# Linear attention groups of a two-block network: one update product for both directions, scores between the updates, outputs beside the scans

## The chip, the cores and the metric

The kernel runs on one core of one Trainium2 chip. Its time is that of the whole program in device microseconds, the median of repeated runs. It is one long program: two layers of a first block (attention and a mixture of experts), then two layers of a second block. The change lies in the second block only.

## The reference, cut to what matters

Each layer of the second block has a mixer. One part of it is gated linear attention over 512 image tokens and 256 context tokens, 6 heads, keys of 32 and values of 64, computed forward and backward in time and added. Tokens are cut into chunks of 16. Decays `b` are running sums inside a chunk:

```python
q_dec = q * jnp.exp(b)
k_inv = k * jnp.exp(-b)
k_end = k * jnp.exp(b_last - b)
a = jnp.where(causal, jnp.einsum('bnihk,bnjhk->bnhij', q_dec, k_inv), 0.0)
o_intra = jnp.einsum('bnhij,bnjhv->bnihv', a, v)
def step(s, xs):
    qd, ke, vv, dec = xs
    o = jnp.einsum('bihk,bhkv->bihv', qd, s)
    s = s * dec[..., None] + jnp.einsum('bjhk,bjhv->bhkv', ke, vv)
    return s, o
```

So each chunk has an update of a 32x64 state per head, a scan runs over the 48 chunks, and a token's output is a part from its own chunk (scores times values) and a part from the state before the chunk. The second layer gives outputs for the 512 image tokens only, the first for all 768. Everything of this part is float32.

## The kernel before, in words

`gated_linear` (L2476) first computes the decayed tensors (`decays`, L2507), and then calls `gla_group` (L2593) twice, once for each three heads. With two layers there are four such groups. A group is a chain of blocks of instructions, and all engines meet at a barrier after each block (`end`, L137), so a group shares no time with what is before or behind it. SyncE issues nothing in a group.

A group of the kernel before has three blocks:

1. `transpose` (L170): `q_dec` and `k_inv` are turned by TensorE into `q_decT` and `k_invT`, tokens along the free axis.
2. The main block (L2641). TensorE, for each of the 6 token tiles of 128 tokens and each of the 3 heads (n = 0 to 17), multiplies an expanded value tile by `k_end`, once for each direction (L2665). The expanded tile `v_chunks` (128x512: the values of the head times a 0/1 mask of the 8 chunks) is made by GpSimd for even n and VectorE for odd n (L2637), into 2 buffers. After each tile, VectorE moves the forward updates of all three heads (96x512) from PSUM into the states (L2713), ScalarE the backward ones (L2748). Then VectorE widens the decays (L2726) and scans (L2733), for one direction and then the other. GpSimd, behind its expansions, clears `q_blocks` (L2646) and fills it with six copies of `q_decT` (L2651). Last, for each output tile TensorE computes scores (L2679), VectorE masks them (L2740), TensorE adds scores times values (L2689) and then 16 products of states and queries, 8 chunks in each of two directions (L2697), and ScalarE copies the tile out (L2752). TensorE waits for both scans before its first product of states.
3. `transpose` again (`oT`, L2755): the outputs are turned back into rows, `gla_rows`.

`gla_output` (L2758) follows after the second group. TensorE runs a float32 matmul as two matmul records in the trace.

Of the kernel before, what the change touches and what calls it, by code (L numbers as in the profile page):

```python
# [11 lines left out]
ALU = mybir.AluOpType  # L12
# [3 lines left out]
P = 128  # L16
# [104 lines left out]
class Program:  # L121
# [2228 lines left out]
    def mixer_layer(self, layer):  # L2350
# [3 lines left out]
        with ExitStack() as outer:  # L2354
# [80 lines left out]
            with ExitStack() as ctx:  # L2435
                ON = self.sbuf(ctx, "gla_rows", [P, upd, GV])
                self.gated_linear(layer, UG, UR, LR, ON, upd)
# [38 lines left out]
    def gated_linear(self, layer, UG, UR, LR, ON, upd):  # L2476
# [10 lines left out]
        with ExitStack() as outer:  # L2487
            with ExitStack() as ctx:
                KE = self.sbuf(ctx, "k_end", [P, NTT, 2, QK])
# [3 lines left out]
                with ExitStack() as c2:  # L2493
                    G = self.sbuf(c2, "log_gate", [P, NTT, 2 * QK])
                    with ExitStack() as c3:
                        ring = self.sbuf(c3, "ring", [P, 1, 2 * QK])
                        self.project(f"z{layer}", ring, [(ins["gla_wg2"][layer], [
                            (G[:, t, d * QK:(d + 1) * QK],
                             [(LR[:, d, t * P:(t + 1) * P], ring[0:GLA_LR + 1, 0, d * QK:(d + 1) * QK])],
                             ("copy", None)) for t in range(NTT) for d in range(2)])])  # L2500

                    self.decays(layer, UG, G, QD, KI, KE, DEC, slot, SL)
                for grp in range(2):
                    self.gla_group(layer, grp, UG, QD, KI, KE, DEC, ON, upd, slot, SL)
            self.gla_output(layer, ON, UR, upd)

    def decays(self, layer, UG, G, QD, KI, KE, DEC, slot, SL):  # L2507
# [3 lines left out]
        with ExitStack() as ctx:  # L2511
# [8 lines left out]
            with nc.Block() as block:  # L2520
                @block.vector
                def _(dve):
# [9 lines left out]
                    for t in range(NTT):  # L2532
                        dve.wait_ge(exps, t + 1)
                        b = t % 2
                        for d in range(2):
# [4 lines left out]
                            ins_ = dve.tensor_tensor(KE[:, t, d, :], E[:, b, 2, c], UG[:, t, QK:2 * QK], ALU.mult)  # L2540
# [52 lines left out]
    def gla_group(self, layer, grp, UG, QD, KI, KE, DEC, ON, upd, slot, SL):  # L2593
# [3 lines left out]
        NC8, W3 = P // CHUNK, HG * GLA_DK  # L2597
# [3 lines left out]
        with ExitStack() as ctx:  # L2601
            QT = self.sbuf(ctx, "q_decT", [W3, 2, upd * P])
            KT = self.sbuf(ctx, "k_invT", [W3, 2, upd * P])

            QB = self.sbuf(ctx, "q_blocks", [W3, 2, upd * NC8, HG, CHUNK])
            ST = self.sbuf(ctx, "states", [W3, 2, GLA_DV, SL])
            DX = self.sbuf(ctx, "decay_wide", [W3, GLA_DV, SL])

            OT = DX[0:GLA_DV, :, :].rearrange("p v s -> p (v s)")[:, 0:HG * upd * P].rearrange(
                "p (h n) -> p h n", h=HG)  # L2610
# [6 lines left out]
            self.transpose(name + "T", groups)  # L2617
# [3 lines left out]
            (updates, up_out_v, up_out_a, cleared, zeroed, blocked, dec_done, scanned, scored, masked, mixed, out_done) = (  # L2621
                sem(n) for n in ("updates", "up_out_v", "up_out_a", "cleared", "zeroed", "blocked", "dec_done",
                                 "scanned", "scored", "masked", "mixed", "out_done"))
            with ExitStack() as c2:
                VX = self.sbuf(c2, "v_chunks", [P, 2, NC8, GLA_DV])
                AT = self.sbuf(c2, "scoresT", [P, 2, HG, 2, P])
                UB = lambda t, d: self.ps[0:W3, 2 * (t % 2) + d, :]
                masks = self.consts[:, self.const_at["upto"][0]:self.const_at["upto"][0] + 2 * P].rearrange(
                    "p (d n) -> p d n", d=2)
                SB = lambda hh: self.ps[:, hh, 0:2 * P]  # L2630
                OB = lambda t: self.ps[0:GLA_DV, 6 + t % 2, 0:HG * P].rearrange("p (h n) -> p h n", h=HG)

                def expand(eng, n):

                    if n >= 2:
                        eng.wait_ge(updates, n - 1)
                    eng.tensor_tensor(VX[:, n % 2], V(n // HG, n % HG).unsqueeze(1).broadcast_to([P, NC8, GLA_DV]),  # L2637
                                      self.const("chunk").unsqueeze(2).broadcast_to([P, NC8, GLA_DV]),
                                      ALU.mult).then_inc(expanded[n % 2], 1)

                with nc.Block() as block:  # L2641
                    @block.gpsimd
                    def _(pool):
                        for n in range(0, NTT * HG, 2):
                            expand(pool, n)
                        pool.memset(QB[:, :, :, :, :], 0.0).then_inc(cleared, 1)  # L2646
                        pool.wait_ge(cleared, 1)
                        for d in range(2):
                            for hh in range(HG):
                                r = slice(hh * GLA_DK, (hh + 1) * GLA_DK)  # L2650
                                pool.tensor_copy(QB[r, d, :, hh, :], QT[r, d, :].rearrange(  # L2651
                                    "p (c n) -> p c n", n=CHUNK)).then_inc(blocked, 1)

                    @block.tensor
                    def _(pe):
                        for t in range(NTT):
                            if t >= 2:
                                pe.wait_ge(up_out_v, t - 1)
                                pe.wait_ge(up_out_a, t - 1)
                            for hh in range(HG):  # L2660
                                n = t * HG + hh
                                pe.wait_ge(expanded[n % 2], n // 2 + 1)
                                for d in range(2):
                                    h = grp * HG + hh
                                    ins_ = pe.matmul(UB(t, d)[hh * GLA_DK:(hh + 1) * GLA_DK, :],  # L2665
                                                     KE[:, t, d, h * GLA_DK:(h + 1) * GLA_DK],
                                                     VX[:, n % 2].rearrange("p c v -> p (c v)"), start=True, stop=True)
                                ins_.then_inc(updates, 1)

                        def scores(t):  # L2670
                            if t == 0:
                                pe.wait_ge(up_out_v, NTT)
                                pe.wait_ge(up_out_a, NTT)
                            else:
                                pe.wait_ge(masked, HG * t)
                            for hh in range(HG):
                                r = slice(hh * GLA_DK, (hh + 1) * GLA_DK)
                                for d in range(2):
                                    ins_ = pe.matmul(SB(hh)[:, d * P:(d + 1) * P], KT[r, d, t * P:(t + 1) * P],  # L2679
                                                     QT[r, d, t * P:(t + 1) * P], start=True, stop=True)  # L2680
                                ins_.then_inc(scored, 1)

                        def mix(t):
                            pe.wait_ge(masked, HG * (t + 1))
                            if t >= 2:
                                pe.wait_ge(out_done, t - 1)
                            for hh in range(HG):
                                for d in range(2):
                                    pe.matmul(OB(t)[:, hh, :], V(t, hh), AT[:, t % 2, hh, d, :],  # L2689
# [368 lines left out]
```

## Time and profile before

| | |
|---|---|
| median of 3 runs | 4325.37 us (4321.52 to 4325.73) |
| the profiled execution: its time | 4329.92 us |
| its span in the trace | 4328.1 us |
| TensorE matmul busy | 3532.5 us (82%), 17678 records |
| VectorE busy | 2639.8 us (61%) |
| ScalarE busy | 2120.1 us (49%) |
| GpSimd busy | 624.3 us (14%) |
| mean granted TensorE clock | 0.899 of full speed |

A row of the timeline gives start, length, engine, line, operation, what is written from what is read, the shapes as output from input, and how many instructions are merged in it; what stands in brackets is how long the engine had been idle before, and who ended that. A granted clock of 1.00 is 2.4 GHz, one of 0.50 is 1.2 GHz; between them is a stretch that had both.

### The profile page before, as it was taken

Reading aid. Unit: us, or ns where it says so; the run is one execution under the profiler, and the core shown is the slowest. Engines: PE = TensorE matmul, PEld = TensorE weight load, DVE = VectorE, ACT = ScalarE, POOL = GpSimd, SP = SyncE. Lnnn points to the kernel's source line nnn. Section 1 sums busy time; section 2 is a strip of 40 time slices with the busy share of each in tenths; the row PEclk is TensorE's granted clock in tenths of the full one; section 3 lists DMA queues with packets and bytes.
Section 4 is the critical chain, followed back from the end, with each engine's and each line's share of the span. In section 5 each row is a group of like instructions: output and inputs, shape, how many; then the busy total and the mean of one; then the engine's idle time right before and its main releaser. Section 6 shows DMA issues by size and latency. Waiting matters only on the chain. (4 is left out here: it accounts for less than half of the span.)

```text
span 4328.1 us, 51356 instructions
## 1 busy us (share of the span) xinstructions
PE 3532.5 (82%) x17678; PEld 2877.1 (66%) x17678; DVE 2639.8 (61%) x3469; ACT 2120.1 (49%) x2670; POOL 624.3 (14%) x266
## 2 busy tenths in 40 slices
PE   6879999657979999487887767999897886568987
PEld 5767777456767777356786455888675785457865
DVE  3659999745479999684654444444345554444545
ACT  2549998634369999573444013333233443034433
POOL 0005333300024343100020320000000021400000
PEclk9879999879979999798998878999998998689998
DMA  3049999720179999581110001111121110012222
GB/s 100 21 150 416 419 417 410 284 61 11 40 272 419 417 415 409 244 369 49 50 48 1 1 32 38 58 68 58 56 61 49 56 50 1 1 44 98 97 78 78
DMA packets 138104, 643.31 MB, mean 149 GB/s; under 512 B 22002, under 2 KB 33620, under 8 KB 74324
## 3 DMA queue, kind: packets, MB, share of 16 engines
q1 hardware_dynamic: 126484, 620.85, 37.2%
q0 software_dynamic: 10080, 16.80, 1.0%
q10 hardware_dynamic: 1392, 3.74, 0.2%
q8 instruction: 86, 1.41, 0.1%
q14 instruction: 62, 0.51, 0.0%
HBM read 636.82 MB, written 24.41 MB: 153 GB/s over the span
## 5 line engine op out<-in xcount | busy, mean ns | idle before, releaser
L1522 DVE TENSOR_TENSOR w_low<-w_raw,w_high 128x2048 fp32r<-128x2048 f32 x392 | 881.8, 2284 | 65.0 <-ACT w_high L1519 60.6
L1519 ACT CAST w_high<-w_raw 128x2048 fp32r<-128x2048 f32 x392 | 746.3, 1910 | 89.5 <-DMA w_raw<-in_moe_down_dram 39.9
L1829 PE MATMUL banks<-w_high,x_split 128*128 128x512 f32 x1024 | 421.6, 412 | 45.7 <-DVE w_low L1522 38.2
L1829 PE MATMUL banks<-w_low,x_split 128*128 128x512 f32 x1024 | 407.7, 398 | 0.0
L534 PE MATMUL banks<-w_high,x_high 128*128 128x512 f32 (+2 forms) x808 | 310.5, 384 | 70.2 <-DVE w_low L455 45.9
L2873 PE MATMUL banks<-x_high,w_high 128*128 128x512 f32 (+1 forms) x1056 | 320.3, 358 | 36.1 <-DVE w_low L2913 36.1
L422 ACT CAST w_high<-w_raw 128x512 fp32r<-128x512 f32 (+2 forms) x200 | 117.8, 589 | 447.6 <-PE banks L534 418.6
L2873 PE MATMUL banks<-x_high,w_low 128*128 128x512 f32 (+1 forms) x1056 | 323.7, 361 | 0.0
L2873 PE MATMUL banks<-x_low,w_high 128*128 128x512 f32 (+1 forms) x1056 | 319.7, 357 | 0.0
L534 PE MATMUL banks<-w_low,x_high 128*128 128x512 f32 (+2 forms) x808 | 302.9, 375 | 0.0
L534 PE MATMUL banks<-w_high,x_low 128*128 128x512 f32 (+2 forms) x808 | 302.7, 375 | 0.0
L1829 PEld LDWEIGHTS banks<-w_high,x_split 128*128 128x128 f32 x1024 | 193.9, 189 | 126.5 <-DVE w_low L1522 82.6
L1779 POOL DMA_INDIRECT expert_rows<-ys,sidx x34 | 257.8, 7581 | 125.4 <-ACT ys L1999 124.4
L711 PE MATMUL banks<-w_high,x_high 128*128 128x512 f32 (+2 forms) x516 | 207.6, 402 | 50.8 <-DVE w_low L683 27.0
L534 PEld LDWEIGHTS banks<-w_high,x_high 128*128 128x128 f32 x808 | 155.6, 193 | 110.9 <-DVE w_low L455 58.3
L453 DVE TENSOR_TENSOR x_low<-mixT,x_high 128x768 fp32r<-128x768 f32 x112 | 107.3, 958 | 194.1 <-ACT x_high L423 194.0
L2873 PEld LDWEIGHTS banks<-x_high,w_high 128*128 128x128 f32 x1056 | 176.5, 190 | 70.2 <-issue 36.8
L1829 PEld LDWEIGHTS banks<-w_low,x_split 128*128 128x128 f32 x1024 | 194.6, 190 | 40.4
L2925 DVE SCALAR_TENSOR_TENSOR convolved<-banks,taps,convolved 128x511 f32<-128x511 f32 (+1 forms) x132 | 82.8, 655 | 207.5 <-ACT convolved L2898 207.5
L711 PE MATMUL banks<-w_low,x_high 128*128 128x512 f32 (+2 forms) x516 | 202.6, 393 | 0.0
L711 PE MATMUL banks<-w_high,x_low 128*128 128x512 f32 (+2 forms) x516 | 202.4, 392 | 0.0
L2898 ACT ACTIVATE convolved<-banks,taps 128x768 f32<-128x768 f32 (+1 forms) x88 | 73.1, 881 | 262.0 <-PE banks L2873 262.0
(392 smaller groups left out, 7596.9 us busy)
## 6 DMA issues: line engine op xcount, KB each, us to landing
w_raw<-in_moe_gate_dram SPq DMA_DIRECT2D x132, 1024.0 KB, 10.5
w_raw<-in_moe_up_dram SPq DMA_DIRECT2D x132, 1024.0 KB, 10.2
w_raw<-in_moe_down_dram SPq DMA_DIRECT2D x132, 1024.0 KB, 11.0
w_raw<-in_w_ada_dram SPq DMA_DIRECT2D x48, 1024.0 KB, 10.7
w_raw<-in_ffn_w_up_dram SPq DMA_DIRECT2D x44, 1024.0 KB
w_raw<-in_ffn_w_down_dram SPq DMA_DIRECT2D x88, 256.0 KB, 2.7
w_raw<-in_w_cols_dram SPq DMA_DIRECT2D x48, 256.0 KB, 2.6
w_raw<-in_w_out_dram SPq DMA_DIRECT2D x32, 256.0 KB, 3.0
```

The source lines that it names most:

```text
L422: act.copy(WS[0][:, rest % S, 0:w], W[:, rest, 0:w])
L453: dve.tensor_tensor(XS[1][:, rest % S, :], x_tile(k), XS[0][:, rest % S, :].bitcast(F32), ALU.subtract)
L534: ins_ = pe.matmul(psum_of(g), st[:, rest % S, a:b], mv[:, rest % S, x:y], start=start and first + second == 0, stop=stop and first == 1)
L711: ins_ = pe.matmul(psum_of(g), XS[first][:, k, t * P:(t + 1) * P], WS[second][:, u % S, 0:w], start=(i == 0 and first + second == 0), stop ...
L1519: act.copy(ex["WS"][0][:, v % HIGH, :], ex["WR"][:, v % RAW, :]).then_inc(ex["high"], 1)
L1522: dve.tensor_tensor(ex["WS"][1][:, v % LOW, :], ex["WR"][:, v % RAW, :], ex["WS"][0][:, v % HIGH, :].bitcast(F32), ALU.subtract).then_inc( ...
L1779: pool.indirect_dma_start(out=Y, out_offset=bass.IndirectOffsetOnAxis(ap=sidx[:, 0:1], axis=0), in_=YS[:, :], in_offset=None, bounds_check ...
L1829: ins_ = pe.matmul(GU[b][m], stationary(b, kk), WS[w][:, s, k * BANK:(k + 1) * BANK], start=(kk == 0 and w == 0), stop=(kk == KD - 1 and w ...
L2873: ins_ = pe.matmul(U(b, ab)[:, x:y], WS[first][:, b, at:at + P], XS[second][:, k, x:y], start=(k == 0 and first + second == 0), stop=(k == ...
L2898: act.activation(Z[:, ab, :], U(b, ab)[:, 0:ntok], ACT.Identity, bias=cv[:, bass.ds(f * 8 + (4 * ab + 3), 1)], scale=cv[:, bass.ds(f * 8 + ...
L2925: dve.scalar_tensor_tensor(out=z[:, x + 1:y], in0=u[:, x:y - 1], scalar=cv[:, bass.ds(f * 8 + 4 * ab, 1)], in1=z[:, x + 1:y], op0=ALU.mult ...
```

## The change

- `k_end` is stored so that for each head the forward and the backward keys (2 x 32 columns) are adjacent. One product with 64 stationary columns gives the updates of both directions of a head: 18 products of a group in place of 36. Each goes to its own bank (4 in turn), forward in partitions 0 to 31, backward in 32 to 63.
- The updates are moved into the states head by head, 32x512 each: 36 moves in place of 12. VectorE makes 6 of them (forward, every third n), ScalarE 30.
- Expanded values have 3 buffers in place of 2; GpSimd expands two of three, VectorE the third. The buffers lie in the three rows of `mixT` that are not in use then.
- The scores of an output tile are computed right behind the updates of that tile, with 4 banks in turn, and masked into a buffer that holds all tiles.
- Each scan is cut in two along the values (24 and 40 of 64). ScalarE widens the decays, the first part at the start of the block.
- `q_blocks` is cleared once per layer, on GpSimd, in the first group's `transpose` block. Its forward copies are made by GpSimd between expansions, the backward ones by ScalarE behind the last move.
- TensorE computes scores times values for all tiles as soon as the updates are placed; the forward products of states for all tiles after the forward scan; the backward ones after the backward scan. Each output tile keeps a bank of its own.
- The rows of a tile are turned back in the same block, behind the backward products of the next tile, and the separate block for it is gone.

The core of the diff:

```diff
-                KE = self.sbuf(ctx, "k_end", [P, NTT, 2, QK])
+                KE = self.sbuf(ctx, "k_end", [P, NTT, GLA_H, 2, GLA_DK])
...
+        VR, UR, SR = 3, 4, 4
...
+            self.transpose(name + "T", groups, clear_blocks if grp == 0 else None)
...
+            parts = [(0, 24), (24, GLA_DV)]
...
+            by_dve = lambda n, d: d == 0 and n % 3 == 0
+            from_pool = lambda n: n % 3 != 2
...
+                @block.gpsimd
+                def _(pool):
+                    for t in range(NTT):
+                        for n in range(t * HG, (t + 1) * HG):
+                            if from_pool(n):
+                                expand(pool, n)
+                        if t % 2 == 1:
+                            pool.wait_ge(expanded[0], expands((t + 1) * HG - 2))
+                            block_q(pool.tensor_copy, 0, t // 2).then_inc(blocked, 1)
+                            pool.wait_ge(blocked, t // 2 + 1)
...
+                    for n in range(N):
+                        pe.wait_ge(expanded[0 if from_pool(n) else 1], expands(n))
+                        if n >= UR:
+                            pe.wait_ge(up_out_v, evacs(n - UR, True))
+                            pe.wait_ge(up_out_a, evacs(n - UR, False))
+                        pe.matmul(UB(n), KE[:, n // HG, grp * HG + n % HG].rearrange("p d k -> p (d k)"),
+                                  VX[:, n % VR].rearrange("p c v -> p (c v)"), start=True, stop=True).then_inc(updates, 1)
+                        if n % HG == HG - 1 and n // HG < upd:
+                            scores(n // HG)
...
+                    pe.wait_ge(masked, upd * HG)
+                    for t in range(upd):
+                        for hh in range(HG):
+                            for d in range(2):
+                                pe.matmul(OB(t)[:, hh, :], V(t, hh), AT[:, t, hh, d, :],
+                                          start=(hh == 0 and d == 0), stop=False, skip_group_check=True)
+                    pe.wait_ge(blocked, HG)
...
+                    pe.wait_ge(scanned, 2)
+                    for t in range(upd):
+                        inter(t, 0)
+                    pe.wait_ge(scanned, 4)
+                    pe.wait_ge(blocked_back, HG)
+                    for t in range(upd):
+                        inter(t, 1).then_inc(mixed, 1)
+                        if t >= 1:
+                            turn_rows(t - 1)
+                    turn_rows(upd - 1)
...
+                    for k in range(4):
+                        d, (a, b) = k // 2, parts[k % 2]
+                        states = ST[:, d, a:b, :].rearrange("p v s -> p (v s)")
+                        dve.wait_ge(widened, k + 1)
+                        dve.tensor_tensor_scan(states, DX[k % 2].rearrange("p v s -> p (v s)"), states, 0.0,
+                                               ALU.mult, ALU.add).then_inc(scanned, 1)
...
+                    widen(0)
+                    for n in range(N):
+                        act.wait_ge(updates, n + 1)
+                        for d in range(2):
+                            if not by_dve(n, d):
+                                place(act.copy, n, d).then_inc(up_out_a, 1)
+                    widen(1)
+                    for hh in range(HG):
+                        block_q(act.copy, 1, hh).then_inc(blocked_back, 1)
+                    for k in (2, 3):
+                        act.wait_ge(scanned, k - 1)
+                        widen(k)
```

## Rows read from the trace of the kernel before

**Rows 1.** The page: the first line of its engine table.

```profile
PE 3532.5 (82%) x17678; PEld 2877.1 (66%) x17678; DVE 2639.8 (61%) x3469; ACT 2120.1 (49%) x2670; POOL 624.3 (14%) x266
```

**Rows 2.** Windows by stage; columns: stretch, length, PE, PEld, DVE, ACT, POOL, clock, DMA.

```profile
2370.00:2399.00 29.00, 22.01 (x72) 6.06 (x72) 13.77 (x17) 3.73 (x6) 12.55 (x10) 1.00 0.00 0
2399.00:2418.00 19.00, 0.73 (x12) 0.56 (x12) 18.90 (x6) 0.00 (x0) 18.76 (x5) 0.62 0.00 1
2418.00:2458.00 40.00, 38.29 (x324) 37.14 (x324) 6.43 (x19) 2.83 (x6) 2.28 (x3) 0.80 0.00 1
```

**Rows 3.** Timeline of the transpose block and the update loop of that group.

```profile
2363.54 1.49 PE L193 MATMUL banks<-consts,q_dec 128*96 128x128 f32 x6 [1.73 <-PEq L139]
...
2369.97 1.04 POOL L2637 TENSOR_TENSOR v_chunks<-u_gla,consts 128x512 f32<-128x512 f32 x1 [122.39 <-SPq L2641]
2371.07 2.45 PE L2665 MATMUL banks<-v_chunks,k_end 128*32 128x512 f32 x8 [2.20 <-POOL v_chunks L2637]
...
2373.55 1.09 DVE L2637 TENSOR_TENSOR v_chunks<-u_gla,consts 128x512 f32<-128x512 f32 x1 [2.00 <-PE banks L2665]
...
2376.09 0.62 ACT L2748 COPY states<-banks 96x512 f32<-96x512 f32 x1 [6.82 <-PE banks L2665]
...
2377.65 0.68 DVE L2713 COPY states<-banks 96x512 f32<-96x512 f32 x1
```

**Rows 4.** Timeline of TensorE in two narrow windows: one and two records begun.

```profile
2374.15 0.62 PE L2665 MATMUL banks<-v_chunks,k_end 128*32 128x512 f32 x1 [0.63 <-POOL v_chunks L2637]
2374.15 1.05 PE L2665 MATMUL banks<-v_chunks,k_end 128*32 128x512 f32 x2 [0.63 <-POOL v_chunks L2637]
```

**Rows 5.** Timeline between the updates and the outputs, same group.

```profile
2395.74 3.93 POOL L2646 MEMSET q_blocks<- 96x4608 f32 x1
...
2399.10 0.73 PE L2679 MATMUL banks<-q_decT,k_invT 32*128 32x128 f32 x12 [0.80 <-DVE states L2713]
...
2401.35 7.18 DVE L2733 TENSOR_TENSOR_SCAN states<-decay_wide,states 96x3136 f32<-96x3136 f32 x1
...
2417.95 1.05 DVE L2740 TENSOR_TENSOR scoresT<-banks,consts 128x256 f32<-128x256 f32 x3
2419.05 1.25 PE L2679 MATMUL banks<-q_decT,k_invT 32*128 32x128 f32 x12 [19.21 <-DVE scoresT L2740]
```

**Rows 6.** Timeline of two output tiles, at the low and the full clock, and the end.

```profile
2420.23 2.82 PE L2689 MATMUL banks<-scoresT,u_gla 128*64 128x128 f32 x12
...
2422.84 3.69 PE L2697 MATMUL banks<-q_blocks,states 96*64 96x48 f32 x32
...
2433.67 1.52 PE L2689 MATMUL banks<-scoresT,u_gla 128*64 128x128 f32 x12
...
2435.03 3.66 PE L2697 MATMUL banks<-q_blocks,states 96*64 96x48 f32 x32
...
2457.38 0.47 ACT L2752 COPY decay_wide<-banks 64x384 f32<-64x384 f32 x1 [5.46 <-PE banks L2697]
...
2458.65 2.15 PE L193 MATMUL banks<-consts,decay_wide 64*128 64x64 f32 x18 [1.31 <-PEq L139]
...
2462.13 1.49 PE L193 MATMUL banks<-consts,q_dec 128*96 128x128 f32 x6 [1.33 <-PEq L139]
```

**Rows 7.** Timeline of the second layer: where its first and second group start and end.

```profile
3644.34 1.04 POOL L2637 TENSOR_TENSOR v_chunks<-u_gla,consts 128x512 f32<-128x512 f32 x1 [104.96 <-SPq L2641]
...
3725.39 1.06 PE L193 MATMUL banks<-consts,q_dec 128*96 128x128 f32 x4 [1.06 <-PEq L139]
...
3730.32 1.04 POOL L2637 TENSOR_TENSOR v_chunks<-u_gla,consts 128x512 f32<-128x512 f32 x1 [36.99 <-SPq L2641]
...
3809.08 1.28 ACT L2794 ACT_TABLE_LOAD   x1 [0.67 <-PEq L139]
```

**Rows 8.** GpSimd's copies of queries by line: least, median and longest, in ns.

```profile
L2651 POOL COPY q_blocks<-q_decT x24: 600/2171/7109, 2399.7 to 3779.3; 32x768 f32<-32x768 f32 x12, 32x512 f32<-32x512 f32 x12
```

**Rows 9.** ScalarE on a larger tile, from the timeline.

```profile
2561.86 2.12 ACT L2794 ACTIVATE u_r<-u_r 128x2304 f32<-128x2304 f32 x1
```

More of the change, by code:

```diff
@@ L2616, in gla_group, with clear_blocks @@
                         groups.append(([src[:, t, d, cols] for t in range(a, b)], dst[:, d, a * P:b * P], None, None))
[L2617 removed]
+            def clear_blocks(pool, done):
+                pool.memset(QB[:, :, :, :, :], 0.0).then_inc(done, 1)
+                pool.wait_ge(done, 1)
+            self.transpose(name + "T", groups, clear_blocks if grp == 0 else None)
             sem = self.Sems(self, name)
             expanded = [sem("expanded_by_pool"), sem("expanded_by_dve")]
[L2621 to L2623 removed]
@@ L2754, in gla_group @@
-            W = HG * GLA_DV
-            self.transpose(name + "oT", [([OT[:, hh, t * P:(t + 1) * P] for hh in range(HG)],
-                                          ON[:, t, grp * W:(grp + 1) * W], None, None) for t in range(upd)])
+            (updates, up_out_v, up_out_a, zeroed, blocked, scanned, scored, masked, mixed, out_done, turned, rows_done) = (
+                sem(n) for n in ("updates", "up_out_v", "up_out_a", "zeroed", "blocked", "scanned", "scored", "masked",
+                                 "mixed", "out_done", "turned", "rows_done"))
@@ new lines, in gla_group, with expand @@
+            ident = self.const("ident")
+            by_dve = lambda n, d: d == 0 and n % 3 == 0
+            evacs = lambda n, dve: sum(1 for m in range(n + 1) for d in range(2) if by_dve(m, d) == dve)
+            from_pool = lambda n: n % 3 != 2
+            expands = lambda n: sum(1 for m in range(n + 1) if from_pool(m) == from_pool(n))
+            def expand(eng, n):
+                if n >= VR:
+                    eng.wait_ge(updates, n - VR + 1)
+                eng.tensor_tensor(VX[:, n % VR], V(n // HG, n % HG).unsqueeze(1).broadcast_to([P, NC8, GLA_DV]),
+                                  self.const("chunk").unsqueeze(2).broadcast_to([P, NC8, GLA_DV]),
+                                  ALU.mult).then_inc(expanded[0 if from_pool(n) else 1], 1)
@@ new lines, in block_q, with place @@
+            def block_q(copy, d, hh):
+                r = slice(hh * GLA_DK, (hh + 1) * GLA_DK)
+                return copy(QB[r, d, :, hh, :], QT[r, d, :].rearrange("p (c n) -> p c n", n=CHUNK))
+            def place(copy, n, d):
+                t, hh = n // HG, n % HG
+                s0 = slot(d, t * NC8) + 1
+                r = slice(hh * GLA_DK, (hh + 1) * GLA_DK)
+                dst = ST[r, 0, :, s0:s0 + NC8] if d == 0 else ST[r, 1, :, s0 - NC8 + 1:s0 + 1][:, :, ::-1]
+                return copy(dst, UB(n)[d * GLA_DK:(d + 1) * GLA_DK].rearrange("p (c v) -> p v c", v=GLA_DV))
@@ L2758, in gla_output @@
+            self.end(sem)
     def gla_output(self, layer, ON, UR, upd):
```

212 lines of the change are left out of this document (83 added, 129 removed).

## The prediction

> **What bounds the kernel now.** I read the page first, then windows by stage, then the timeline of one group. The page has TensorE busy for 82% of the span [rows 1], which says nothing of this change: a group is closed by barriers, so each microsecond of it counts in full, whoever is busy. The windows show three stages of a group in the first layer [rows 2]. For 29 us updates are made. For 19 us TensorE stands (0.73 us busy) while VectorE is busy for 18.90. For 40 us TensorE is busy for 38.29 and the others wait. So the stages have different bounds, and they stand one behind the other.
>
> In the update loop two products, one even n and one odd, repeat every 3.08 us (2371.07 in [rows 3] to 2374.15 in [rows 4]), of which TensorE works 2.45. What sets it is the buffer: an expansion of 1.04 must end before its products, about 2 us for the first of two that share TensorE, and only then may the buffer be written again. Eighteen products make nine such rounds, 28 us, and a hand-off.
>
> In the scan stage VectorE runs a widening and a scan, twice: two scans of 7.18 [rows 5] and 4.5 for the widenings, by the 18.90 of [rows 2]. In these 19 us TensorE could have computed scores times values, but its next instruction waits for masks that stand behind the scans on VectorE.
>
> In the output stage a tile costs 0.73 to 1.25 for scores, 1.4 to 2.6 for scores times values, 3.65 for the products of states [rows 5, 6].
>
> **The change part by part.** Times are from the first expansion of a block; the group of reference is the first.
>
> *Update products.* Two records of one product that write the same columns of the array start 0.43 us apart (1.05 - 0.62, [rows 4]). The new product has two records: 2 x 0.43 = 0.86 us. The bounds: half of 2.45 would be 1.22 for two, so 0.61 each; at the half clock 1.71. I take 0.86. The Trainium skill (TensorE: Matmul & The Clock Gate, "Part 3: Packing small matmuls — row/col tiling") says that matmuls of few stationary columns run side by side when their outputs lie in different groups of 32 partitions. That speaks against this change: before, successive heads lay in different groups and overlapped (eight records in 2.45 us where eight pitches of 0.43 are 3.4), now all lie in partitions 0 to 63. By the rule the gain of halving the calls is 0.73 us for two products and not 1.23; the trace agrees.
>
> *The loop's round.* For three heads TensorE needs 3 x 0.86 and the scores of the tile, 0.73 at the full clock [rows 5]: 3.31. Beside it ScalarE moves five times 32x512. The row for 96x512 is 0.62 [rows 3]; its length should be set by the 512 elements: 3.1. VectorE: one move 0.68, one expansion 1.09, three masks 1.05 [rows 3, 5]: 2.8. GpSimd: two expansions 2.1, and a query copy in every second round. Such a copy takes 0.6 to 7.1 us [rows 8]; the long ones stand beside a scan, which this loop has not, and the median is 2.2. I take 0.6 to 2.2: in two rounds 4.2 + 2.2 = 6.4 against 6.6. Nobody exceeds TensorE, but all four are close, so I add 1 us for waits. The buffers no longer bound: 3 of them carry 1.04 + 0.86 per 3.31.
>
> Sum to the last placed update: 1.1 hand-off [rows 3], five rounds 16.55, three products 2.6, end of the last record 0.2, ScalarE's backlog and last two moves 1.6, waits 1.0 = 23.0. Before: 2369.97 to 2399.1 [rows 3, 5] = 29.1. Gain 6.1. The other groups start at the low clock, where scores cost 1.25 in place of 0.73 [rows 5]; I give them 1.5 for that, 24.5, and take off 1.2 in the second layer, which has scores in four of six rounds: 23.3.
>
> *Clearing and the layout of k_end.* The clearing of 3.93 us [rows 5] goes to GpSimd in a transpose block of 6.4 us (2363.54 to 2369.97, [rows 3]) in which GpSimd was idle: nothing; uncovered it would be at most 4 us a layer. `k_end` is written in runs of 32 in place of 192; I expect no change. No row of the groups above shows such a write; the nearest is the expansion, 1.09 for 512 elements, so some 0.4 for 192, and 24 writes would cost 10 us if they doubled and nothing if not.
>
> *Scans.* VectorE now only scans: 14.4 us for both, each cut 3:5 (2.7 and 4.5), the fixed part of two more instructions 0.1 each. ScalarE widens at about 0.92 ns an element (2.12 for 2304, [rows 9]): 1.1 and 1.8 us. The second part ends 1.8 after placing, before scan 2.7 asks for it; three query copies of about 0.85 end at 4.4, the third widening at 5.5, the fourth, which waits for the second scan at 7.2, at 9.0, and scan four begins at 9.9. So the scans run without a gap: forward done at 7.2, backward at 14.5.
>
> *Outputs, first layer.* From the last placed update: masks 0.4; scores times values for six tiles, 1.4 (full, 2433.67 to 2435.03) to 2.6 (low, 2420.23 to 2422.84) each [rows 6]. The clock was 1.00 in the loop and fell to 0.50 in the idle scan stage (0.62 in its mean, [rows 2]); now TensorE goes on without a break, so I lean to the fast side: 1.7, sum 10.2. It is later than 7.2, so the forward scan is hidden. Then 12 half tiles of states at 1.81 (3.69 and 3.66 for the 32 records of both halves at the low and the full clock, less the end of the last record, [rows 6]): 21.8. The backward scan (14.5) is hidden too, for TensorE comes to it at 21.5. Row turns: 18 calls took 2.15 [rows 6], 0.35 a tile, five on TensorE's path 1.7. Behind the last: copy 0.5, turn 0.6, move 0.4, hand-offs 0.2 = 1.7. Barrier 0.9. Sum 36.7, where before 2399.1 to 2462.13 = 63.0 [rows 5, 6]. Gain 26.3. Late now is TensorE alone.
>
> *Outputs, second layer.* Four tiles: 0.4 + 6.8 = 7.2, level with the forward scan; half tiles 4 x 1.81 = 7.2, to 14.4, level with the backward scan; then 7.2 + 3 turns 1.0 + 1.7 + 0.9. Sum 25.3.
>
> Groups: in the first layer 23.0 + 36.7 = 59.7 against 92.1 (2369.97 to 2462.13), gain 32.4; its second, priced alike and late by 1.5 before as after, the same. In the second layer 23.3 + 25.3 = 48.6 against 81.1 and 78.8 (3644.34 to 3725.39, 3730.32 to 3809.08, [rows 7]): 32.5 and 30.2. Sum 127.5. I take off 2 for the writes of `k_end`. The profiled execution took 4329.9, so 4204.4 by its clock; it lies 4.5 above the median of the runs, so 4200 as a median.
>
> **A second rule.** The query copies on GpSimd last up to 7.1 us where the scans run [rows 8]. The Trainium skill (SBUF — State Buffer, "Who interferes with whom") says that a VectorE instruction with two SBUF inputs keeps a GpSimd instruction that reads SBUF out until it ends. The trace agrees as far as it goes. By it an expansion or copy of the new loop could wait up to one VectorE expansion of 1.1 us; this is rival B's mechanism.
>
> **The rivals.**
>
> A, *the low clock stays*. If TensorE had 1.2 GHz all through the block, a round would be 3 x 1.71 + 1.25 = 6.4, 3.1 longer, 18 us a group; scores times values 5.4 more in a group of the first layer, 3.6 in the second. 4 x 18 + 2 x 5.4 + 2 x 3.6 = 90 us lost: 4290. For it: the clock was low in parts of the output stage with TensorE busy nearly throughout (0.80 in the mean, [rows 2]). Against: it was 1.00 in the loop at 22 of 29 us busy [rows 2], and the new loop is busier.
>
> B, *the loop is bound by the helpers*. Four engines need 2.8 to 3.3 us in a round of 3.3 and wait for each other; GpSimd behind VectorE's two-input instructions would have 2 x 1.4 + half of 2.2 = 3.9, with stalls a round of 4.5. 1.2 x 24 rounds = 29 us: 4229. For it: VectorE's expansion is stretched beside GpSimd (1.09, against 0.68 for a move of as many elements, [rows 3]). Against: GpSimd's own 1.04 never moves.
>
> C, *better than priced*. Products overlap in part as before (0.61) and a round takes 2.7, with moves on ScalarE that overlap a little: 0.6 x 24 = 14 us; scores times values at the full clock, 1.4: 4 us. 4200 - 18 = 4182.
>
> D, *slower than before*. Moves of 32 partitions whose source and target start at different partitions, in reverse order for half of them, are in no row; their bound from below is 0.62, from above I have none nearer than the scan's 7.18. They are 30 on ScalarE in place of 6. The gain is gone when a round takes 3.3 + 125.5 / 24 = 8.5 us, when one such move takes 1.7 us. Every copy of this trace goes by its free length, so this is unlikely.
>
> **How the numbers follow.** Forecast 0.62 (4200, own range 4190 to 4215), C 0.14, B 0.16, A 0.05, D 0.03, of which 0.01 is within 0.2%. Range 4178 to 4236: it takes in C and B and the bound of `k_end`, and leaves out A and D. A measurement of this kernel can tell 0.2%, 8.6 us. Faster 0.96, same 0.01, slower 0.03.
>
> **What would show it.** In the trace after: product records 0.43 apart at clock 1.00; the block's first expansion to the last placed update in 23 us; four scans, 2.7, 4.5, 2.7, 4.5, without a gap; the first products of states about 10 us after the last placed update in the first layer and 7 in the second; no transpose block behind. It is wrong if a round takes over 4 us, if scan three or four starts late behind a widening, or if 16 products of states for a half tile take other than 1.8 us.

## The result, and the profile after

The changed kernel takes 4191.86 us (median of 4 runs, 4183.98 to 4201.06) against 4325.18 for the kernel before. The ratio is 0.9694, with a 95% interval of 0.9674 to 0.9715. The forecast was 4200, with 4178 to 4236 as its range. Run again beside some of the kernels below it took 4188.84 (4185.43 to 4196.68) beside 4322.50, ratio 0.9696 (0.9679 to 0.9712).

The page of the changed kernel, first line of its engine table, answers to [rows 1]:

```profile
PE 3484.8 (83%) x17534; PEld 2845.6 (68%) x17534; DVE 2606.3 (62%) x3467; ACT 2211.5 (53%) x2784; POOL 579.4 (14%) x264
```

As before, the page does not tell where the time went: TensorE's busy time fell by 48 us and the span by 138. The windows do. These are the stages of the first layer's first group (loop, scores times values, products of states), in the columns of [rows 2]:

```profile
2364.80:2389.80 25.00, 22.24 (x109) 7.96 (x110) 15.91 (x32) 19.87 (x32) 15.85 (x15) 0.93 0.00 1
2389.80:2397.60 7.80, 7.80 (x72) 7.80 (x73) 7.80 (x3) 6.25 (x6) 0.00 (x0) 1.00 0.00 0
2397.60:2422.40 24.80, 24.79 (x209) 23.68 (x207) 6.96 (x6) 3.61 (x7) 0.00 (x0) 0.58 0.01 1
```

The 19 us in which TensorE stood are gone. In the second stage VectorE scans while TensorE is busy for all 7.80 us. ScalarE has gone from 3.73 to 19.87 us in the loop and comes next behind TensorE.

The timeline of the changed kernel's loop, one round of three heads, answers to [rows 3, 4]:

```profile
2374.25 0.73 PE L2693 MATMUL banks<-q_decT,k_invT 32*128 32x128 f32 x12
2374.36 0.99 DVE L2655 TENSOR_TENSOR mixT<-u_gla,consts 128x512 f32<-128x512 f32 x1 [0.86 <-PE banks L2702]
2374.91 2.79 PE L2702 MATMUL banks<-mixT,k_end 128*64 128x512 f32 x6
2375.27 1.07 DVE L2758 TENSOR_TENSOR scoresT<-banks,consts 128x256 f32<-128x256 f32 x3
2376.07 2.04 POOL L2655 TENSOR_TENSOR mixT<-u_gla,consts 128x512 f32<-128x512 f32 x2 [1.27 <-PE banks L2702]
2376.26 0.67 DVE L2670 COPY states<-banks 32x512 f32<-32x512 f32 x1
2376.88 3.17 ACT L2670 COPY states<-banks 32x512 f32<-32x512 f32 x5 [0.21 <-PE banks L2702]
2377.63 0.73 PE L2693 MATMUL banks<-q_decT,k_invT 32*128 32x128 f32 x12
```

A round is 3.38 us (2374.25 to 2377.63), and TensorE has no idle time in it. The timeline of the same group's scans and outputs answers to [rows 5, 6]:

```profile
2389.76 8.04 PE L2713 MATMUL banks<-scoresT,u_gla 128*64 128x128 f32 x72 [1.24 <-DVE scoresT L2758]
2389.76 2.60 DVE L2767 TENSOR_TENSOR_SCAN states<-decay_wide,states 96x1176 f32<-96x1176 f32 x1 [0.15 <-ACT states L2670]
...
2392.29 4.21 DVE L2767 TENSOR_TENSOR_SCAN states<-mixT,states 96x1960 f32<-96x1960 f32 x1
...
2396.42 2.58 DVE L2767 TENSOR_TENSOR_SCAN states<-decay_wide,states 96x1176 f32<-96x1176 f32 x1
...
2397.64 14.40 PE L2719 MATMUL banks<-q_blocks,states 96*64 96x48 f32 x128
2398.92 4.21 DVE L2767 TENSOR_TENSOR_SCAN states<-mixT,states 96x1960 f32<-96x1960 f32 x1
...
2411.97 0.58 PE L2729 MATMUL banks<-consts,k_invT 64*128 64x64 f32 x3
2412.07 0.47 ACT L2797 COPY k_invT<-banks 64x384 f32<-64x384 f32 x1 [1.31 <-PE banks L2719]
2412.47 2.02 PE L2719 MATMUL banks<-q_blocks,states 96*64 96x48 f32 x16
...
2414.43 0.58 PE L2729 MATMUL banks<-consts,k_invT 64*128 64x64 f32 x3
...
2424.23 1.49 PE L193 MATMUL banks<-consts,q_dec 128*96 128x128 f32 x6 [1.21 <-PEq L139]
```

The four scans follow each other, and TensorE is never idle from 2389.76 to the last turn. In the second layer the scans do bound, for a moment; this is its first group. The first scan there waits for ScalarE's last moves, and TensorE then waits 1.57 us for the forward scan:

```profile
3587.99 5.71 ACT L2670 COPY states<-banks 32x512 f32<-32x512 f32 x9 [0.20 <-PE banks L2702]
...
3593.80 5.42 PE L2713 MATMUL banks<-scoresT,u_gla 128*64 128x128 f32 x48 [2.42 <-issue]
3593.92 2.60 DVE L2767 TENSOR_TENSOR_SCAN states<-decay_wide,states 96x1176 f32<-96x1176 f32 x1 [3.53 <-ACT states L2670]
...
3600.80 10.91 PE L2719 MATMUL banks<-q_blocks,states 96*64 96x48 f32 x96 [1.57 <-DVE states L2767]
```

Group times, from the first expansion to the first instruction behind the group (L1, L2: layer; a, b: group), with the part up to the first scan:

| kernel | L1a | L1b | L2a | L2b | sum | to first scan, L1a |
|---|---|---|---|---|---|---|
| before | 92.2 | 93.0 | 81.1 | 78.8 | 345.0 | 31.4 |
| after | 59.4 | 59.0 | 50.5 | 50.1 | 219.0 | 24.9 |
| after, again | 58.8 | 58.9 | 49.4 | 49.5 | 216.6 | 24.3 |
| e1, two products apart | 59.1 | 58.8 | 48.9 | 49.3 | 216.0 | 24.6 |
| e2, same columns | 74.0 | 74.1 | 63.1 | 63.2 | 274.3 | 39.3 |
| e3, outputs behind scans | 74.2 | 75.3 | 62.9 | 63.2 | 275.5 | 24.3 |
| e4, scores behind updates | 63.7 | 62.6 | 49.5 | 49.5 | 225.3 | 26.9 |
| e5, rows in own block | 58.2 | 58.4 | 49.6 | 49.9 | 216.1 | 24.3 |
| e6, two buffers | 60.1 | 58.6 | 49.8 | 49.7 | 218.2 | 25.4 |
| e7, widening on VectorE | 59.8 | 60.4 | 52.9 | 53.0 | 226.1 | 25.1 |
| e8, column halves | 57.6 | 60.5 | 49.3 | 48.9 | 216.4 | 23.2 |
| e10, halves and moves | 57.2 | 58.6 | 45.9 | 46.1 | 207.7 | 22.5 |
| e11, before with three buffers | 85.4 | 84.8 | 69.2 | 66.8 | 306.2 | 23.1 |
| e12, combined | 57.1 | 58.6 | 46.2 | 47.5 | 209.3 | 22.4 |

So the groups lost 126 to 128 us, and the medians differ by 133. The table is of single profiled executions. In them the time outside the groups is 3983.2 us before and 3970.9 and 3968.0 us in the two traces of the changed kernel. In the traces of its variants it is 3969.4 to 3981.1 us, in e11, which has the old groups, 3982.3 us. The code out there is the same but for the writes of `k_end` and the clearing in the first `transpose` block of a layer. The last run below comes back to this.

### The profile page after: what moved, and what is told of

It reads as the page before. It is cut to its first block and busy times, and to the rows that moved or that the text cites. A ratio compares the mean times of both kernels' runs of the same rounds, so it can differ in the third digit from the quotient of the medians.

```text
span 4189.9 us, 51108 instructions
## 1 busy us (share of the span) xinstructions
PE 3484.8 (83%) x17534; PEld 2845.6 (68%) x17534; DVE 2606.3 (62%) x3467; ACT 2211.5 (53%) x2784; POOL 579.4 (14%) x264
## 5 line engine op out<-in xcount | busy, mean ns | idle before, releaser
L534 PEld LDWEIGHTS banks<-w_high,x_high 128*128 128x128 f32 x808 | 155.9, 193 | 109.4 <-DVE w_low L455 57.6
```

The lines of the kernel that those rows point to most:

```text
L534: ins_ = pe.matmul(psum_of(g), st[:, rest % S, a:b], mv[:, rest % S, x:y], start=start and first + second == 0, stop=stop and first == 1)
```

## The experiments

All are the changed kernel with one edit, but for e10 and e12, which join several, and e11, which is an edit of the kernel before. No run is called e9. They ran in three sets, e1 to e4, e5 to e8 and the rest, each set on one chip, where the kernel before took 4319.07, 4323.14 and 4322.50 us.

**e1: two products, columns apart.**

```diff
-                        pe.matmul(UB(n), KE[:, n // HG, grp * HG + n % HG].rearrange("p d k -> p (d k)"),
-                                  VX[:, n % VR].rearrange("p c v -> p (c v)"), start=True, stop=True).then_inc(updates, 1)
+                        for d in range(2):
+                            ins_ = pe.matmul(UB(n)[d * GLA_DK:(d + 1) * GLA_DK], KE[:, n // HG, grp * HG + n % HG, d],
+                                             VX[:, n % VR].rearrange("p c v -> p (c v)"), start=True, stop=True)
+                        ins_.then_inc(updates, 1)
```

> The changed kernel with two products of 32 stationary columns for each head in place of one of 64; the forward one writes partitions 0 to 31, the backward one 32 to 63 of the same bank, so their columns of the array differ. Theory (work in different column groups overlaps, work in the same one does not): four records in about 0.9 to 1.0 us, a round of three heads stays at 3.4 to 3.6 us, the whole at 4192 to 4200 us. Rival (what counts is the number of products, so that one product was the gain of the loop): 1.72 us a head, a round of 5.9, 2.5 x 24 rounds = 60 us more, 4252 us.

Measured: 4185.29 us (4183.51 to 4190.33), no slower than with one product. Four records took as long as two:

```profile
2378.93 2.77 PE L2703 MATMUL banks<-mixT,k_end 128*32 128x512 f32 x12
```

**e2: two products, same columns.**

```diff
-        VR, UR, SR = 3, 4, 4
+        VR, UR, SR = 3, 2, 4
...
-            UB = lambda n: self.ps[0:2 * GLA_DK, n % UR, :]
+            UB = lambda n, d: self.ps[0:GLA_DK, 2 * (n % UR) + d, :]
```

The two products are those of e1, written to `UB(n, 0)` and `UB(n, 1)`.

> As the run before it, but both products write partitions 0 to 31, of two banks, so with two heads in flight in place of four. Theory (same columns: one behind the other): 1.72 us a head, a round of 5.9 us with the scores, 60 us more than the changed kernel, 4252 us; the moves (1.25 a head) stay hidden. Rival (columns do not matter): the same time as the run with the columns apart.

Measured: 4251.76 us (4249.29 to 4255.76), 66 more than e1 by the medians and 58 more by the groups. The first scan comes at 39.3 us in place of 24.6. Twelve records of e2, against the same twelve of e1 above:

```profile
2377.70 5.34 PE L2703 MATMUL banks<-mixT,k_end 128*32 128x512 f32 x12
```

It is 0.445 us a record against 0.23. The number of products does not count here; which columns they write does. e2 also has two heads in flight where e1 has four, but TensorE shows no idle time in those 5.34 us, so the columns set it.

**e3: outputs behind the scans.**

```diff
                     pe.wait_ge(masked, upd * HG)
+                    pe.wait_ge(scanned, 4)
```

> The changed kernel, but TensorE waits for all four scans before the first product of scores and values. Theory (outputs beside the scans is the largest term): 13.8 us more in each group, and scores times values then starts at the low clock after the idle stretch, up to 1.2 us a tile more: 7 in a group of the first layer, 5 in one of the second. Together 55 (clock stays) to 79 us (clock falls) more: 4247 to 4271 us. Rival (TensorE bounds the rest anyway and the overlap is worth little): under 20 us more.

Measured: 4254.94 us (4250.11 to 4265.20), 63 and 66 more than the changed kernel's two medians (4191.86 and 4188.84), inside the expected band; the groups sum to 56 and 59 more. From the trace of e3:

```profile
2401.64 10.00 PE L2714 MATMUL banks<-scoresT,u_gla 128*64 128x128 f32 x72 [14.77 <-DVE states L2768]
```

In the changed kernel this wait was 1.24 us. The 72 records take 10.00 us where they took 8.04, at a clock that fell meanwhile: 0.50 in the wait and 0.80 in the mean over these records. The two windows of e3:

```profile
2391.00:2401.00 10.00, 0.00 (x0) 0.00 (x0) 10.00 (x3) 4.19 (x4) 0.00 (x0) 0.50 0.00 0
2401.60:2411.50 9.90, 9.86 (x73) 9.89 (x74) 0.00 (x0) 0.00 (x0) 0.00 (x0) 0.80 0.01 2
```

**e4: scores and masks behind all updates.**

```diff
-                        if n % HG == HG - 1 and n // HG < upd:
-                            scores(n // HG)
+                    for t in range(upd):
+                        scores(t)
```

VectorE's masks likewise stand behind its last move.

> The changed kernel with all scores and masks behind the last update product. Theory: the loop then goes by ScalarE's five moves, 3.1 us a round in place of 3.38 (1.7 less a group in the first layer, 1.1 in the second), and the masks, 0.36 us each on VectorE and 18 or 12 of them, stand between the last product and the outputs and scans: 6.5 and 4.3 us, of which 1.1 was there before. Net 3.5 us a group, 14 in all: 4206 us. Rival (scores between updates cost as much in the loop as they save behind it): 4192 within 4 us.

Measured: 4202.17 us (4197.58 to 4205.63), 10 to 13 more. The groups took 63.7, 62.6, 49.5 and 49.5 us: 4 more in the first layer, nothing in the second. I had expected 3.5 in each. In the first layer the first scan comes at 26.9 us, 2 later, and the 72 records of scores times values take 10.18 us in place of 8.04, at a mean clock of 0.78. In the second layer the first scan comes at 24.4 us, as in the changed kernel, and the clock is 1.00. The traces show why the masks cost nothing there. Without scores in the loop the last product ends at 19.8 us, in both layers. The masks of the first layer need 6.5 us from there, those of the second 4.07. In the second layer of the changed kernel the last product ends at 21.8 to 22.9 us, and the scan then waits some 2.4 us more for ScalarE's moves, so it comes no earlier.

**e5: rows in a block of their own.** The turns leave the block (`turn_rows` and VectorE's copies are gone), and `self.transpose(name + "oT", ...)` follows it, from outputs kept in `scoresT`.

> The changed kernel with the rows turned back in a block of their own behind it, as before the change. Theory, from the trace of the changed kernel: a tile with a turn in it starts every 2.46 us where the products of states alone take 1.81, so five turns cost 3.2 us of TensorE's path in a group of the first layer and three cost 1.9 in one of the second; the last copy to the next block is 1.8 us with turns inside and was 4.3 with the block. Net -0.7 in the first layer, +0.5 in the second, in all within 2 us of the changed kernel: 4190 to 4194 us. Rival (the block that went was worth what it took, 3.3 us with its barrier): 13 us more, 4205.

Measured: 4191.54 us (4187.75 to 4196.52), no change. Beside the changed kernel's second trace the groups of the first layer are 0.4 to 0.6 us shorter, those of the second 0.2 to 0.4 longer. A half tile with a turn in it starts every 2.46 us (2411.97 to 2414.43 above), and in e5 copies follow each other every 1.78 us.

**e6: two buffers.**

```diff
-        VR, UR, SR = 3, 4, 4
+        VR, UR, SR = 2, 4, 4
```

> The changed kernel with two buffers of expanded values in place of three. Theory (the third buffer matters, but a product of 0.86 in place of about 2 leaves the two far less bound): a buffer's turn is 1.04 + 0.15 + 0.86 = 2.05 us for two heads, 3.1 a round, with the scores partly inside its waits: a round of 3.6 to 4.2 in place of 3.38, 5 to 20 us more in all, 4197 to 4212. Rival (buffers were the bound before and are now not): no change.

Measured: 4195.79 us (4191.81 to 4202.19), 4 and 7 more than the changed kernel's two medians, which is within the scatter. The groups sum to 218.2 us against 216.6 and 219.0 with three buffers. The third buffer matters little here. A round did grow, though by less than I said (scores 2377.77, 2381.46 and 2384.98 in its trace, so 3.69 and 3.52 in place of 3.38). In the second layer the last product ends at 23.1 us in place of 21.8 (second trace of the changed kernel), but ScalarE's moves behind it cover that.

**e7: widening on VectorE.**

```diff
-                        dve.wait_ge(widened, k + 1)
+                        dve.tensor_copy(DX[k % 2], DEC[:, d, grp, :].unsqueeze(1).broadcast_to(
+                            [W3, b - a, SL])).then_inc(widened, 1)
+                        dve.wait_ge(widened, k + 1)
```

ScalarE's four widenings are gone.

> The changed kernel with the four widenings on VectorE before each scan part. They take 0.9 and 1.5 us. Theory (first layer bound by TensorE, second by the scans until the forward one is done): forward scan done at 9.2 us after placing in place of 6.9. First layer: scores times values end at 7.9, so 1.3 more a group, and the backward scan stays hidden. Second layer: 2.3 more for the forward and 1.9 for the backward one, 4.2 a group. Together 11 us more: 4203. Rival (scans are hidden everywhere): no change.

Measured: 4204.46 us (4198.66 to 4207.79), 13 and 16 more than the changed kernel's two medians, near the 11 expected; sum of groups 226.1, so 7 to 9.5 more, of which 5.3 to 7 in the second layer. TensorE waits for the forward scan there for 3.51 us in place of 1.57, and a second time for the backward one:

```profile
3615.00 7.34 PE L2719 MATMUL banks<-q_blocks,states 96*64 96x48 f32 x64 [3.51 <-DVE states L2769]
...
3623.55 1.69 PE L2719 MATMUL banks<-q_blocks,states 96*64 96x48 f32 x13 [1.21 <-DVE states L2769]
```

**e8: column halves.**

```diff
-            UB = lambda n: self.ps[0:2 * GLA_DK, n % UR, :]
+            UB = lambda n: self.ps[64 * (n % 2):64 * (n % 2) + 2 * GLA_DK, n % UR, :]
```

> The changed kernel, but successive heads write partitions 0 to 63 and 64 to 127 in turn, so that their products use different columns. Theory (columns apart overlap): TensorE needs less than 3.38 a round, ScalarE's five moves of 0.62 then set it at 3.1 to 3.2: 0.2 x 24 = 5 to 7 us less, 4186 us. Rival (one stream of 512 columns at a time): no change.

Measured: 4189.05 us (4187.59 to 4196.38), which tells nothing from the changed kernel. The loop did as expected: ScalarE's 29 moves stand back to back, and the first scan comes at 23.2 to 23.9 us in place of 24.3 to 25.4. From the trace of e8:

```profile
2368.72 18.55 ACT L2670 COPY states<-banks 32x512 f32<-32x512 f32 x29 [0.76 <-PE banks L2702]
```

But in its second group TensorE then waited 2.72 us for ScalarE, and scores times values took 10.92 us in place of 8.04, at a mean clock of 0.73 in place of 1.00. The gain of that group was given back there. The length of the wait alone does not decide it: in the first group TensorE waited 2.71 us and kept the full clock. These are the lines of both groups and the window of the second:

```profile
2387.36 8.05 PE L2713 MATMUL banks<-scoresT,u_gla 128*64 128x128 f32 x72 [2.71 <-ACT states L2670]
...
2451.32 10.92 PE L2713 MATMUL banks<-scoresT,u_gla 128*64 128x128 f32 x72 [2.72 <-ACT states L2670]
```

```profile
2451.40:2462.00 10.60, 10.60 (x72) 10.60 (x73) 10.19 (x4) 7.09 (x6) 0.00 (x0) 0.73 0.01 2
```

**e10: halves and more moves on VectorE.** As e8, and:

```diff
-            by_dve = lambda n, d: d == 0 and n % 3 == 0
+            by_dve = lambda n, d: d == 0 and (n % 3 == 0 or n >= HG * upd or n >= N - 2)
```

> The changed kernel with successive heads in different halves of the partitions, and with the forward moves of the last two heads (in the second layer of the last six) on VectorE. Theory (with the halves ScalarE's moves are the bound: in the run with the halves alone 29 of them stand back to back for 18.55 us): first layer two moves less, 1.2 us a group; second layer four moves less and the last placed update right behind the last product, 2 us a group. 6 us less than with the halves alone, 12 less than the changed kernel: 4180 us. Rival (the last moves are hidden behind masks on VectorE): as with the halves alone, 4187.

Measured: 4187.29 us (4182.10 to 4193.78) beside 4188.84 for the changed kernel on the same chip. Its profiled groups sum to 207.7 us against 216.6, 3.5 less in each of the second layer; I had expected 12 less in all. In the first layer TensorE waits 2.21 us for masks in place of 1.24. Its trace has 3976.5 us outside the groups against 3968.0, and the medians do not show these 9 us beyond their scatter.

**e11: the kernel before with three buffers.**

```diff
-                    if n >= 2:
-                        eng.wait_ge(updates, n - 1)
+                    if n >= 3:
+                        eng.wait_ge(updates, n - 2)
```

The buffers are, as in the changed kernel, in the free rows of `mixT`.

> The kernel before the change, with three buffers of expanded values in place of two (in the free rows of mixT), and nothing else. Theory (the buffer's turn of 1.04 + 2 us sets the 3.08 us of a pair of heads, and heads whose outputs lie in different columns overlap): a pair takes 2.2 to 2.5 us, 5 to 8 us less a group, 20 to 30 in all: 4290 to 4300 us beside 4320 for the kernel before. So most of the gain of the changed loop would be the buffer's. Rival (TensorE's 2.45 and its waits for moved banks set the pair): under 5 us in all.

Measured: 4287.58 us (4280.13 to 4290.27), ratio to the kernel before 0.9913 (0.9896 to 0.9929): 35 us less. In the first group the first scan comes at 23.1 us in place of 31.4, so nine pairs of heads are 8.2 us shorter. TensorE's products now follow each other without a wait, 72 records in 19.08 us, 2.1 us a pair in place of 3.08. In the second layer a group is 12 us shorter. From the trace of e11:

```profile
2371.39 19.08 PE L2665 MATMUL banks<-mixT,k_end 128*32 128x512 f32 x72 [2.20 <-POOL mixT L2637]
```

**e12: e10, scores times values from the masks on, forward scan behind the forward moves.**

```diff
-            OB = lambda t: self.ps[0:GLA_DV, t, 0:HG * P].rearrange("p (h n) -> p h n", h=HG)
+            OB = lambda t: self.ps[0:GLA_DV, (4 + t) % 8, 0:HG * P].rearrange("p (h n) -> p h n", h=HG)
...
-                    dve.wait_ge(up_out_a, evacs(N - 1, False))
+                    dve.wait_ge(up_out_a, evacs(14, False) - 1)
```

TensorE waits for the placed updates only before the fifth output tile (in the second layer the fourth), and VectorE for all of ScalarE's moves only before the backward scan.

> As the run with halves and moves, and further: output tiles 0 to 3 get the banks of the scores, so that scores times values start when the masks are done and not when all updates are placed; and the forward scan waits for the forward moves only. Theory (first layer bound by TensorE from there on, second by the scans): first layer 1.3 less a group for TensorE's earlier start, second layer 0.6 for the earlier scan. 4 us less than without the two, 16 less than the changed kernel: 4176 us. Rival (no more to be had from the seam between the stages): as the run without them.

Measured: 4187.71 us (4185.55 to 4192.52), no better than e10; groups 209.3. The step from the loop to the outputs had nothing more to give. In the first layer TensorE waits 2.13 us for the masks of the last tile, which now stand behind the moves that I had given to VectorE. In the second layer scores times values start earlier, but TensorE then waits 3.61 us for the forward scan.

```profile
2385.06 2.12 DVE L2670 COPY states<-banks 32x512 f32<-32x512 f32 x3
...
2387.21 1.09 DVE L2759 TENSOR_TENSOR scoresT<-banks,consts 128x256 f32<-128x256 f32 x3
...
2388.35 8.07 PE L2714 MATMUL banks<-scoresT,u_gla 128*64 128x128 f32 x72 [2.13 <-DVE scoresT L2759]
```

So no version was shown to beat the changed kernel.

**The changed kernel again.**

> The changed kernel again, unchanged, on the same chip as the other three. All theories: 4184 to 4201 us as measured, and the four groups at 59.4, 59.0, 50.5 and 50.1 us within 1 us. If the 12 us by which its profiled run was faster outside the groups are scatter, the first group's start (2364.8 in that run, 2370.0 before) will move by some us between runs; if they come from the change, it stays at 2365 within 1 us.

Measured: the first group starts at 2362.8 us. In the other variants of the changed kernel it starts between 2362.4 and 2374.3, in the kernel before at 2370.0 and in e11 at 2370.3, though the program is the same to that point but for the writes of `k_end` and, with the new groups, the clearing. Among the variants alone the start moves by 12 us, and this is scatter. Whether a few of the 5 to 7 us outside the groups come from the change stays open: the part behind the last group took 519.0 and 517.2 us with the old groups (before, e11) and 513.2 to 516.2 us in all twelve traces with the new ones, and no run was made on that.

## Why the prediction was right

*The loop.* The product record spacing was right: 2.79 us for six records is 0.43 each and the end of the last, at clock 1.00. A round was 3.38 against 3.31, plus 1 for waits in all. To the first scan it took 24.9 us where I had 23.0 in the first group. I had given only the later groups a start at the low clock; the first had it too. Its mean was 0.72 from 2364.80 to 2370.87, where the first scores came, 2.3 us later than by my sum. This was the mis-sized term. The other groups' 24.9, 25.4 and 25.1 stand against 24.5, 23.3 and 23.3: in the second layer I had taken off 1.2 for missing scores, but ScalarE's nine moves (5.7 us for the last two rounds) bound there, so nothing came off.

*What in the loop did it.* I named the buffer as the bound of the old loop, and e11 shows it: one more buffer alone takes 7 to 12 us off a group. After the change the third buffer matters little (e6). That this is because a product now holds its buffer for 0.86 us and not for 2 was argued and not tried by itself. The new loop is not shorter than that of e11 (24.9 us to the first scan against 23.1, of which 2.3 are the widening on VectorE), but it holds the scores as well. That one product took the place of two is worth nothing by itself: e1 has two, with their columns apart, and is as fast. The rule of column groups was rightly weighed; its other half, that e1's layout would have done as well, I had not drawn. e2 gives the price of the wrong columns: 58 us in the groups, 66 by the medians.

*Scans.* 2.60, 4.21, 2.58, 4.21 without a gap, where I had 2.7 and 4.5. In the second layer the forward scan made TensorE wait 1.57 us, where I had the two level.

*Outputs.* In the first layer scores times values took 7.9 us to the first product of states, against 10.2: the clock stayed at 1.00, as rival C had it. TensorE stopped there for only 1.24 us, and in all seven traces with this wait in the first layer (both of the changed kernel, e1, e2, e5, e6, e7) the clock was 1.00 behind it. In the second layer it stopped for 2.4 us, and there it was not sure: in the second trace of the changed kernel the 48 records of the first group took 7.09 us at a mean clock of 0.76, where the first trace has 5.42 at 1.00. It cost nothing there, since the wait for the forward scan was gone.

```profile
3591.27 7.09 PE L2713 MATMUL banks<-scoresT,u_gla 128*64 128x128 f32 x48 [2.41 <-issue]
3598.27 10.92 PE L2719 MATMUL banks<-q_blocks,states 96*64 96x48 f32 x96
```

The half tile was 1.80 (14.40 for 128 records, eight of them) against 1.81. A turn cost 0.65 on TensorE's path (2.46 less 1.81) and not 0.35, and e5 shows that moving the turns into the block gained nothing. Together 34.5 and 34.1 against 36.7, and 25.1 against 25.3 in the second layer. e3 shows the term that carries the change: without the overlap 56 to 59 us come back in the groups, 63 to 66 by the medians.

*The sum.* 126.0 us in the groups against 127.5. The four loops took 6.2 us more than priced and the four output parts 5.3 us less; that the two made up for each other is luck. The 2 us for the writes of `k_end` did not come (0.36 each, as before), and neither did a cost of the clearing: GpSimd's 3.94 us stand in a `transpose` block of 6.47 us, where it took 6.46. The profiled execution, 4191.66 us where my sum gave 4204.4, owes this difference to what lies outside the groups, which the prediction did not have.

*The rivals.* A (low clock throughout) did not come: 0.93 in the loop. It was right for the products of states (0.58), which cost the same at either clock. B (helpers bound the round) did not come in a round like the one shown, where TensorE has no idle time; in the last two rounds of the second layer it did, by ScalarE. ScalarE is so near elsewhere that TensorE's gain in the loop ends there (e8). B's other mechanism cost little: beside VectorE's expansion a query copy took 1.16 us in place of 0.81. VectorE was the one stretched: in e11 its 18 expansions that began while GpSimd was idle took 0.69 us each, and in the kernel before the 35 that began beside an instruction of GpSimd took 0.93 to 1.42. C came in its second part only, and that part was added wrongly: 0.3 us less for each of 20 tiles is 6 us, not 4. D: a move of 32 partitions took 0.62 on ScalarE like one of 96.

## What to carry to other kernels

Before halving a number of matmuls, look at which columns of the array they write: here products in different groups of 32 output partitions overlapped already, and merging them gained nothing. Where a loop waits, work out the turn of one buffer (fill, use, release) against the busy time of each engine; here a third buffer alone took 35 us off the kernel before. The largest part came from order: work that needs no scan goes beside the scan. It also spared the clock: behind a wait of 1.24 us TensorE ran scores times values at 1.00, behind one of 14.77 us (e3) at 0.80. Taken out one at a time, the overlap with the scans (e3), the scores between the updates (e4) and the widening on ScalarE (e7) cost 66, 13 and 16 us over 4188.84. That is 95 of the 99 us that lie between e11 and the changed kernel. Whether they simply add was not tried, and nor were the moves head by head and the earlier query copies by themselves.

## What the runs showed of the hardware that was not expected

- TensorE fully busy does not mean the full clock: in 24.80 us of products of 96x64 with 48 columns it was busy for 24.79 at a mean clock of 0.58, right after 1.00 for scores times values.
- A scan cut in two takes less than the whole: 2.60 + 4.21 = 6.81 us against 7.18, with one instruction more. Before, GpSimd copied beside it, and now it does not. That this is the cause is likely but not shown: in the second layer of the kernel before, where GpSimd's copies are of 32x512 and not of 32x768, the same whole scan took 6.98 us.

```profile
3674.57 18.76 POOL L2651 COPY q_blocks<-q_decT 32x512 f32<-32x512 f32 x5
3676.22 6.98 DVE L2733 TENSOR_TENSOR_SCAN states<-decay_wide,states 96x3136 f32<-96x3136 f32 x1
```

- In the loop GpSimd's copies of 32x768 took 0.81 to 1.16 us; none of the 2 to 7 us of [rows 8] came back. From the trace of the changed kernel:

```profile
2378.18 1.16 POOL L2662 COPY q_blocks<-q_decT 32x768 f32<-32x768 f32 x1
```
